# Values and gate of a retention layer as seven block products

## The chip, the cores and the metric

The kernel is one program on one core of a Trainium2 chip. It is written instruction by instruction: each engine (TensorE, ScalarE, VectorE, GpSimd, and SyncE for loads) has a program of its own, and semaphores order them. The metric is the time on the device in microseconds. GpSimd is called POOL, VectorE DVE, ScalarE ACT and TensorE PE in the profile.

## The reference, cut to what matters

A sequence of 512 tokens of width 1024 goes through a retention layer, an attention layer and a third block of pooling, neighbourhood attention and a large MLP. The change is in the first layer:

```python
def _retention_layer(x, w_in, w_out):
    hproj = x @ w_in                       # 512 x 1024 by 1024 x 6144
    q, k = 4 heads of 256 each; v, gate = 4 heads of 512 each
    q = _rope(q); k = _rope(k) * DK_A ** -0.5
    o = _chunkwise_retention(q, k, v)      # causal scores times a decay, times v
    o = (o - mean(o)) * rsqrt(var(o) + 1e-5)
    return (o * silu(gate)) @ w_out
```

The kernel computes each float32 product as three matmuls: both operands are split into a high part, rounded to the format TensorE takes, and a low part, the remainder; then high times high, high times low and low times high are added up (`split_dots`, L565 to L569).

## The kernel before

**A head.** Weights come as panels of 128x2048 floats, six a head: query, key, two of values, two of gate (`split_hi`, `split_lo`; `A0 + 0` to `A0 + 5`). SyncE loads a panel into `stage[p % 2]` (L580). ScalarE rounds it in two halves of 128x1024 into `whi` (L1458), once TensorE has finished the panel before the last, which lay in the same buffer; GpSimd subtracts and writes the remainder `wlo` (L724). TensorE's program for a head: the query product and the key product (48 matmuls of 512 columns each), the values (`token_tiles`, 96), the scores (24, of 512 to 128 columns), the first half of the gate (48), the inner products scores times values (30), the second half of the gate (48), and 16 transposes of the normalised result. Gate and result meet after the transposes, with features on partitions.

**VectorE in a head**, in this order: turning of the query by the rotary tables (`work`, four products with a PSUM source L2399 to L2402, one subtraction L2404 and one addition L2405 with both sources in SBUF), remainders of the rounded query `qk_lo`, the same for the key, remainders of the values, scores times decay (L2417), remainders of the scores `s_lo`, gate (L2426), statistics (L2433 to L2438), normalisation (L2447), products with the gate (L2452). Remainders are all recorded at L2082, roundings by ScalarE at L1461.

**Behind the heads** comes the output layer AO, which already goes by seven block products of two steps each, d = 0 to 13 (`seven`, 24 matmuls each). Its weight sums are made in DRAM by GpSimd's adding DMAs (`sum_step`) upon copies that ScalarE's queue issues (`copy_blocks`). Remainders of its steps 0 and 1 are GpSimd's work (L758, L765), of all later ones VectorE's. Then the layer norm, and the rest of the kernel, which the change leaves as it is but for the copies and sums that prepare the MLP's weights (`copy_b11`, `copy_b22`, `up_sum`).

The order of work on every engine is the order of the program; nothing is planned at run time. An engine that waits for a semaphore holds back all that stands behind it in its program.

## Time and profile before

| | |
|---|---|
| median of 3 runs | 1414.61 us (1414.3 to 1414.74) |
| the profiled execution | 1414.12 us, its span 1412.3 us |
| TensorE busy (matmul) | 1393.4 us, 99% |
| VectorE busy | 919.2 us, 65% |
| ScalarE busy | 698.8 us, 49% |
| GpSimd busy | 388.2 us, 27% |
| granted TensorE clock, mean | 0.997 |
| first layer's heads | 19.2 to 319.4 us |

A busy share is of the whole span. A matmul of 512 columns stands with 0.39 us in the timeline, since matmuls overlap; what it costs is the distance from its start to that of the next. "x2" in a timeline is two instructions merged, with the time of both; what stands in brackets is the idle time before and what ended it.

### The profile page before, as it was taken

What the parts mean: (1) busy time and instruction counts of PE and PEld (TensorE: products, weight loads), DVE (VectorE), ACT (ScalarE), POOL (GpSimd) and SP (SyncE); (2) the same over time, 40 slices, a digit from 0 to 9 for tenths busy, and PEclk for the clock granted to TensorE, in tenths of its full rate; (3) what the DMA queues carried; (4) which work ended last, traced back from release to release, by engine and by line L of the source; (5) the groups of instructions that cost most, each with busy time, mean ns of one, the idle gap of its engine ahead of it and who ended that gap; (6) DMA issues with size and microseconds to landing.
All of it is one profiled execution on the core that took longest, in us unless ns stands there. A gap on an engine that the chain in (4) does not pass through costs nothing.

```text
span 1412.3 us, 19358 instructions
## 1 busy us (share of the span) xinstructions
PE 1393.4 (99%) x7412; PEld 1203.4 (85%) x7412; DVE 919.2 (65%) x1562; ACT 698.8 (49%) x1131; POOL 388.2 (27%) x192
## 2 busy tenths in 40 slices
PE   9999999999999999999999999999999899999998
PEld 7888888888889888888888888778888899998887
DVE  6444354549961865545544479946877878789896
ACT  4323232236554533443443356648956465666554
POOL 5334254541034343343334230035314100000000
PEclk9999999999999999999999999999999999999999
DMA  7257946946533988975796557353122576446552
GB/s 292 90 194 204 296 155 164 263 115 258 188 103 129 289 235 221 312 176 157 210 302 161 162 207 284 135 193 126 64 83 75 165 184 173 128 173 213 197 187 111
DMA packets 53890, 260.26 MB, mean 184 GB/s; under 512 B 5568, under 2 KB 10304, under 8 KB 28224
## 3 DMA queue, kind: packets, MB, share of 16 engines
q1 hardware_dynamic: 37152, 163.04, 33.3%
q0 software_dynamic: 5760, 41.95, 14.9%
q10 hardware_dynamic: 10912, 54.40, 11.3%
q8 instruction: 41, 0.67, 0.2%
q14 instruction: 25, 0.20, 0.0%
HBM read 252.03 MB, written 91.23 MB: 243 GB/s over the span
## 4 chain that ended last, share of the span: by engine, by line
PE 89%; DVE 7%; ACT 2%; POOL 1%; issue 1%; DMA 0%; SPq 0%; DVEq 0%; ACTq 0%; POOLq 0%
PE bank L567 23%; PE bank L569 23%; PE bank L568 23%; PE bank L1176 6%; PE bank L1238 4%; PE bank L1127 3%; PE bank L1155 1%; DVE wlo L2082 1%; DVE wlo_a L2082 1%; DVE xlo L2082 1%; DVE br_lo L2082 1%; PE bank L1318 0%; PE bank L913 0%; PE bank L1015 0%; DMA stage<-in_w 0%
## 5 line engine op out<-in xcount | busy, mean ns | idle before, releaser
L724 POOL TENSOR_TENSOR wlo<-stage,whi 128x1024 fp32r<-128x1024 f32 (+2 forms) x116 | 291.9, 2543 | 544.8 <-ACT whi L1458 544.8
L1458 ACT ACTIVATE whi<-stage 128x1024 fp32r<-128x1024 f32 (+2 forms) x120 | 122.2, 1069 | 87.3 <-PE bank L569 64.3
L567 PE MATMUL bank<-xhi,whi 128*128 128x512 f32 (+1 forms) x428 | 149.3, 349 | 3.2 <-DVE xlo L2082 1.8
L569 PE MATMUL bank<-xhi,wlo 128*128 128x512 f32 (+1 forms) x428 | 148.5, 347 | 0.0
L568 PE MATMUL bank<-xlo,whi 128*128 128x512 f32 (+1 forms) x428 | 148.3, 346 | 0.0
L1461 ACT ACTIVATE whi<-stage 128x1024 fp32r<-128x1024 f32 (+2 forms) x125 | 118.0, 989 | 40.3 <-PE bank L569 29.4
L2082 DVE TENSOR_TENSOR wlo<-stage,whi 128x1024 fp32r<-128x1024 f32 x108 | 123.4, 1168 | 14.7 <-ACT whi L1461 14.7
L567 PEld LDWEIGHTS bank<-xhi,whi 128*128 128x128 f32 x428 | 81.1, 189 | 13.5 <-issue 2.2
L567 PE MATMUL bank<-whi,xhi 128*128 128x512 f32 (+1 forms) x236 | 91.4, 387 | 1.1 <-POOL wlo L724 1.1
L569 PE MATMUL bank<-whi,xlo 128*128 128x512 f32 (+1 forms) x236 | 90.4, 383 | 0.0
L568 PE MATMUL bank<-wlo,xhi 128*128 128x512 f32 (+1 forms) x236 | 90.3, 383 | 0.0
L569 PEld LDWEIGHTS bank<-xhi,wlo 128*128 128x128 f32 x428 | 81.0, 189 | 10.3
L568 PEld LDWEIGHTS bank<-xlo,whi 128*128 128x128 f32 x428 | 81.1, 189 | 9.8
L2082 DVE TENSOR_TENSOR wlo_a<-stage,whi_a 128x1024 fp32r<-128x1024 f32 (+1 forms) x60 | 71.4, 1217 | 18.5 <-ACT whi_a L1461 18.5
L1461 ACT ACTIVATE whi_a<-stage 128x1024 fp32r<-128x1024 f32 (+1 forms) x56 | 53.8, 1008 | 22.8 <-PE bank L569 19.9
L567 PEld LDWEIGHTS bank<-whi,xhi 128*128 128x128 f32 x236 | 44.8, 190 | 10.4 <-POOL wlo L724 1.3
L569 PEld LDWEIGHTS bank<-whi,xlo 128*128 128x128 f32 x236 | 44.7, 190 | 8.4
L568 PEld LDWEIGHTS bank<-wlo,xhi 128*128 128x128 f32 x236 | 44.9, 190 | 8.0
L1176 PE MATMUL bank<-xhi,whi 128*128 128x512 f32 x128 | 50.7, 396 | 0.0
L1176 PE MATMUL bank<-xhi,wlo 128*128 128x512 f32 x128 | 50.0, 391 | 0.0
L1176 PE MATMUL bank<-xlo,whi 128*128 128x512 f32 x128 | 49.9, 390 | 0.0
L2082 DVE TENSOR_TENSOR pt_lo<-bank,pt_hi 128x384 fp32r<-128x384 f32 (+1 forms) x48 | 26.6, 595 | 34.9 <-ACT pt_hi L1461 34.9
(451 smaller groups left out, 3943.5 us busy)
## 6 DMA issues: line engine op xcount, KB each, us to landing
stage<-in_w SPq DMA_DIRECT2D x79, 1024.0 KB, 4.9
tsum<-in_w ACTq DMA_DIRECT2D x32, 1024.0 KB, 14.5
stage<-tsum SPq DMA_DIRECT2D x32, 1024.0 KB, 4.8
tsum<-in_w POOLq DMA_DIRECT2D x16, 1024.0 KB, 10.1
tsum<-tsum POOLq DMA_DIRECT2D x16, 1024.0 KB, 10.1
stage<-in_w SPq DMA_DIRECT2D x8, 1152.0 KB, 6.3
usum<-in_w POOLq DMA_DIRECT2D x8, 1024.0 KB, 9.9
stage<-usum SPq DMA_DIRECT2D x32, 256.0 KB, 3.8
```

What stands on the lines that cost most here:

```text
L567: pe.matmul(dst, a_hi, b_hi, start=start, stop=False)
L568: pe.matmul(dst, a_hi, b_lo, start=False, stop=False)
L569: return pe.matmul(dst, a_lo, b_hi, start=False, stop=stop)
L724: pool.tensor_tensor(lo[:, r], stage[p % 2][:, r], hi[:, r].bitcast(F32), ALU.subtract).then_inc(w_lo, 1)
L1127: last = pe.matmul(bank[4 + q][:, 0:w], left, right, start=i == 0, stop=i == 4)
L1155: last = pe.transpose(dst[min(kt, 2)][:, at:at + P], prob[:, src:src + P], ident[:, :])
L1176: last = pe.matmul(bank[0][:, :], left[:, k, f], right[:, k, :], start=i == 0, stop=i == 23)
L1238: last = pe.matmul(bank[m][:, :], left[:, k, m * P:(m + 1) * P], right[:, k, :], start=i == 0, stop=i == 23)
L1458: act.activation(parts(p)[0][:, r], stage[p % 2][:, r], ACT.Copy).then_inc(w_hi, 1)
L1461: act.activation(dst, src, ACT.Copy, scale=scale).then_inc(signal, 1)
L2082: dve.tensor_tensor(dst, src, hi.bitcast(F32), ALU.subtract).then_inc(signal, 1)
```

## The change

The values and the gate of a head are one product of x (512x1024) with a 1024x1024 weight, values on the left and gate on the right. The change cuts x into blocks of 256 tokens by 512 inputs and the weight into blocks of 512x512: B11 and B21 (values), B12 and B22 (gate). Seven block products take the place of eight: with B11 and B21 directly, with B22, and with four sums T1 = B12 - B11, T3 = B22 - B12, T2 = B22 - T1, T4 = B21 - T2. The four sums of x that they need (`operand_sums`) are made once, in head 0. A block product is 24 matmuls of 512 columns.

- Per head VectorE makes the four weight sums, 128x2048 each, and the remainders of T1 to T4; GpSimd makes those of query, B11, key, B21 and B22. Products are combined by VectorE in `kept1` and `gate`, now with tokens on partitions.
- TensorE's order in a head: B11, key, B21, B22, scores (last block first), T1, T2, T3, T4, inner products, query of the next head, transposes. The last head's transposes come behind step 1 of AO.
- The gate is multiplied in with the centring of the result (`onorm`); ScalarE then scales by the root, and copies the transposed result out.
- The loads follow the new order and new places (`a_stage`); loops over heads are written out; the copies and sums in DRAM are spread otherwise: `copy_b22` goes one by one behind steps 4 to 11 of AO, `up_sum` behind AO's step 1, and the load of x to the last head. ScalarE rounds AO's first two operands within the last head, ahead of T3.

Core of the diff (TensorE's head first):

```diff
+            def head(h):
+                if h:
+                    pe.wait_ge(a_c, 12 * h)
+                block_product(h, A_B11, X)
+                turned_product(h, AK)
+                pe.wait_ge(a_k1, 2 * h + 2)
+                block_product(h, A_B21, X, True)
+                pe.wait_ge(a_q32, 4 * h + 3)
+                if h == 0:
+                    pe.wait_ge(vs_l, 1)
+                block_product(h, A_B22, Y)
                 pe.wait_ge(a_qklo, 4 * h + 4)
+                if h:
+                    pe.wait_ge(a_ot, 4 * h)
+                for kt in S_ORDER:
...
+                pe.wait_ge(a_vlo, 4 * h + 2)
+                if h == 0:
+                    pe.wait_ge(vs_l, 4)
+                block_product(h, A_T1, X)
+                pe.wait_ge(a_dec, 4 * h + 2)
+                block_product(h, A_T2, Z)
+                pe.wait_ge(a_dec, 4 * h + 4)
+                block_product(h, A_T3, W)
+                pe.wait_ge(a_c, 12 * h + 4)
+                block_product(h, A_T4, X)
...
+                pe.wait_ge(a_slo, 4 * h + 4)
+                pe.wait_ge(a_c, 12 * h + 6)
+                inner(0, (0,))
+                inner(1, (0, 1))
+                inner(2, (0, 1))
+                inner(3, (0, 1))
+                pe.wait_ge(a_vlo, 4 * h + 3)
+                inner(2, (2,))
+                pe.wait_ge(a_vlo, 4 * h + 4)
+                inner(3, (2, 3))
...
+            for h in range(HA):
+                head(h)
+                if h + 1 < HA:
+                    pe.wait_ge(a_c, 12 * h + 10)
+                    turned_product(h + 1, AQ)
+                    turn_head(h)
```

GpSimd and ScalarE:

```diff
+            for h in range(HA):
+                for j in BY_POOL:
+                    if (h, j) == (0, AQ):
+                        continue
+                    head_lo(h, j)
...
+            operand_lo(AO, 0)
+            operand_lo(AO, 1)
             weights_lo(AO, 0)
...
+                head_hi(h, AK, (a_ld[1], 32 * h + 16), (a_qk, 4 * h + 2))
+                if h:
+                    turned_out(h - 1)
...
+                head_hi(h, A_B21, (a_ld[3], 16 * h + 16), (a_m, 7 * h + 1))
+                if h == 0:
+                    operand_sum_hi(3, 3)
...
+                head_hi(h, A_B22, (a_ld[0], 32 * h + 32), (a_qk, 4 * h + 4))
...
+                if h == HA - 1:
+                    act.wait_ge(a_ot, 4 * h)
+                    operand_hi(AO, 0)
+                    operand_hi(AO, 1)
+                head_hi(h, A_T3, (g_sum, 3 + 4 * h + 2), (a_m, 7 * h + 4))
...
+                tanh(0)
+                tanh(1)
+                if h + 1 < HA:
+                    head_hi(h + 1, AQ, (a_ld[0], 32 * h + 48), (a_m, 7 * h + 6))
```

VectorE:

```diff
+                rope(h, 0)
+                if h == 0:
+                    operand_sums()
+                rope_lo(h, 0)
+                if h == 0:
+                    for n in range(4):
+                        operand_sum_lo(n)
+                rope(h, 1)
+                t1()
+                rope_lo(h, 1)
+                for q in range(2):
+                    v_low(q, X[q][:, :])
+                both(A_T1)
+                t3()
+                dve.wait_ge(g_dlo, 8 * h + 2)
+                dve.tensor_tensor(s0, s2, s0, ALU.subtract).then_inc(g_sum, 1)
...
+                for i in range(TT):
+                    decays(h, i)
...
+                both(A_T2)
...
+                dve.tensor_tensor(s0, a_staged(h, A_B21), s0, ALU.subtract).then_inc(g_sum, 1)
+                both(A_T3)
...
+                for a in range(2):
+                    dve.tensor_tensor(kept1[:, a, :], kept1[:, a, :], Z[a][:, :], ALU.add).then_inc(a_c, 1)
...
+                both(A_T4)
...
                 gates(0)
                 gates(1)
+                dve.wait_ge(a_m, 7 * h + 7)
+                for a in range(2):
+                    dve.wait_ge(a_c, 12 * h + a + 7)
+                    dve.tensor_tensor(kept1[:, a, :], kept1[:, a, :], X[a][:, :], ALU.add).then_inc(a_c, 1)
+                for q in range(2, TT):
+                    dve.wait_ge(a_c, 12 * h + 9 + q)
+                    v_low(q, kept1[:, q - 2, :])
+                gates(2)
+                gates(3)
+                if h == HA - 1:
+                    combine(AO, 2)
...
+                for q in range(TT):
+                    dve.scalar_tensor_tensor(out=onorm[:, q, :], in0=B[q][:, :], scalar=mv[:, q, 0:1],
+                                             in1=gate[:, q, :], op0=ALU.subtract, op1=ALU.mult).then_inc(a_on, 1)
```

Here `rope` is the turning with its four products, subtraction and addition, `both` the two halves of a panel's remainders, and `head_hi` waits for a load or a sum and for TensorE, then rounds a panel.

## Rows read from the trace of the kernel before

**Rows 1.** TensorE's waits: the longest in 0 to 325 us, and the longest of the run.

```profile
PE bank L1025 <- ACT xhi L1461: 1.6, 1, 1.6
...
PE bank L913 <- DVE h_tok L2263: 2.0, 1, 2.0
```

**Rows 2.** TensorE's timeline: start us, us, engine, line, operation.

```profile
107.91 0.39 PE L567 MATMUL bank<-whi,xhi 128*128 128x512 f32 x1
...
129.67 0.39 PE L567 MATMUL bank<-qk_hi 128*128 128x512 f32 x1
...
133.44 0.44 PE L567 MATMUL bank<-xhi,whi 128*128 128x512 f32 x1
...
330.40 0.39 PE L567 MATMUL bank<-whi_a,s_hi 128*128 128x512 f32 x1
```

**Rows 3.** A stretch of heads 1 and 2: busy us of each engine, TensorE clock, DMA.

```profile
core 0: us, PE busy (x) PEld busy (x) DVE busy (x) ACT busy (x) POOL busy (x), PEclk, DMA share, GB/s
...
150.00:200.00 50.00, 50.00 (x231) 41.56 (x230) 25.17 (x34) 14.34 (x18) 20.50 (x9) 1.00 0.68 233
```

**Rows 4.** VectorE's timeline, turning queries in heads 0, 1 and 2.

```profile
21.94 0.69 DVE L2404 TENSOR_TENSOR work<-work 128x512 f32<-128x512 f32 x1
22.55 0.69 DVE L2405 TENSOR_TENSOR work<-work 128x512 f32<-128x512 f32 x1
...
97.23 0.69 DVE L2399 TENSOR_TENSOR work<-bank,rope_a 128x512 f32<-128x512 f32 x1 [8.98 <-PE bank L569]
...
99.75 1.64 DVE L2404 TENSOR_TENSOR work<-work 128x512 f32<-128x512 f32 x1
101.31 2.88 DVE L2405 TENSOR_TENSOR work<-work 128x512 f32<-128x512 f32 x1
...
175.03 0.69 DVE L2399 TENSOR_TENSOR work<-bank,rope_a 128x512 f32<-128x512 f32 x1 [8.98 <-PE bank L569]
```

**Rows 5.** GpSimd's timeline in head 1.

```profile
98.43 5.21 POOL L724 TENSOR_TENSOR wlo<-stage,whi 128x1024 fp32r<-128x1024 f32 x2 [7.50 <-ACT whi L1458]
...
120.19 4.77 POOL L724 TENSOR_TENSOR wlo<-stage,whi 128x1024 fp32r<-128x1024 f32 x2 [4.89 <-ACT whi L1458]
```

**Rows 6.** VectorE's timeline near 1092 us.

```profile
1091.93 1.22 DVE L2082 TENSOR_TENSOR s2u_lo<-hid,s2u_hi 128x1024 fp32r<-128x1024 f32 x1
1093.12 3.36 DVE L2082 TENSOR_TENSOR dr_lo<-hid,dr_hi 128x1024 fp32r<-128x1024 f32 x1
1096.41 3.40 DVE L2082 TENSOR_TENSOR xlo<-hid,xhi 128x1024 fp32r<-128x1024 f32 x1
```

**Rows 7.** GpSimd's timeline, the same stretch.

```profile
1092.14 3.26 POOL L849 TENSOR_TENSOR hid<-hid 128x1024 f32<-128x1024 f32 x1 [2.49 <-DVE hid L2287]
```

**Rows 8.** VectorE's timeline in a layer norm.

```profile
400.58 2.03 DVE L2256 SCALAR_TENSOR_TENSOR xres<-oT,small,rows 128x1024 f32<-128x1024 f32 x1
```

**Rows 9.** GpSimd's timeline, the same stretch.

```profile
395.78 5.75 POOL L724 TENSOR_TENSOR wlo<-stage,whi 128x1024 fp32r<-128x1024 f32 x2 [70.45 <-ACT whi L1458]
```

**Rows 10.** VectorE's timeline, undisturbed instructions of 128x1024.

```profile
336.99 1.22 DVE L2082 TENSOR_TENSOR wlo<-stage,whi 128x1024 fp32r<-128x1024 f32 x1
338.12 1.21 DVE L2097 TENSOR_TENSOR oT<-oT 128x1024 f32<-128x1024 f32 x1
```

**Rows 11.** ScalarE's groups, 0 to 420 us: count, busy us, mean ns.

```profile
L1458 ACT ACTIVATE whi<-stage 128x1024 fp32r<-128x1024 f32 x50 | 50.1, 1053 | 68.6 <-PE bank L569 59.4 <-DMA stage<-in_w 6.2 <-issue 3.0
```

**Rows 12.** Panel loads of L580, 0 to 60 us: issue to landing.

```profile
DMA to landing us min/median/max: 4.8/5.0/10.4
```

**Rows 13.** VectorE's timeline, statistics and normalisation of head 1.

```profile
151.42 0.70 DVE L2433 BATCH_NORM_STATS2 stat<-bank 128x6 f32<-128x512 f32 x1 [2.02 <-PE bank L569]
...
153.81 2.97 DVE L2447 TENSOR_SCALAR work<-bank,mv,small 128x512 f32<-128x512 f32 x4
```

**Rows 14.** TensorE's timeline, its first matmuls.

```profile
1.47 3.78 PE L982 MATMUL bank<-qk_lo 128*128 128x512 f32 x8 [1.47 <-DVE qk_lo L2371]
5.09 0.91 PE L1025 MATMUL bank<-xhi,whi 128*128 128x512 f32 x2
```

More of the change, by code:

```diff
@@ L336, in program @@
         a_on = sem("a_on")
+        a_m = sem("a_m")
         a_t = sem("a_t")
@@ new lines, in turned_product @@
+            def turned_product(h, j):
+                wh, wl = [w.rearrange("p (k n) -> p k n", k=KX) for w in a_parts(h, j)]
+                if h and j == AK:
+                    pe.wait_ge(a_ot, 4 * h - 2)
+                for m in range(2):
+                    c = slice(m * P, (m + 1) * P)
+                    for k in range(KX):
+                        if m == 0 and k in (0, KX // 2):
+                            head_need(h, j, k > 0)
+                        last = split_dots(pe, (W if j == AQ else Y)[m][:, :], wh[:, k, c], wl[:, k, c], xhi[:, k, :],
+                                          xlo[:, k, :], k == 0, k == KX - 1)
+                    last.then_inc(a_qk, 1)
@@ new lines, in block_product @@
+            def block_product(h, j, banks, onto=False):
+                wh, wl = [w.rearrange("p (k n) -> p k n", k=PK) for w in a_parts(h, j)]
+                x_hi, x_lo = a_operand(j)
+                for kk in range(PK):
+                    if kk % 2 == 0:
+                        head_need(h, j, kk > 0)
+                    for a in range(2):
+                        r = slice(a * P, (a + 1) * P)
+                        last = split_dots(pe, banks[a][:, :], x_hi[:, kk, r], x_lo[:, kk, r], wh[:, kk, :], wl[:, kk, :],
+                                          kk == 0 and not onto, kk == PK - 1, onto)
+                last.then_inc(a_m, 1)
@@ L1623, in _, with head_hi @@
             act.wait_ge(f_hi, 5)
-            act.sem_inc(w_hi, 2)
-            split_hi(A0 + 1)
-            act.wait_ge(xt_lo, KX)
-            act.dma_start(xres[:, :, :], t["x"]).then_inc(aux["x"], 16)
+            act.sem_inc(g_hi, 2)
             A, B, E, O = bank[0:4], bank[4:8], bank[0::2], bank[1::2]
-            def head(h, last=False):
-                n = 6 * h
-                act.wait_ge(a_dec, 4 * h + 4)
+            X = bank[0:2]
+            def head_hi(h, j, ready, count):
+                act.wait_ge(*ready)
+                act.wait_ge(*count)
+                for b in range(2):
+                    r = slice(b * PAN // 2, (b + 1) * PAN // 2)
+                    copy(a_parts(h, j)[0][:, r], a_staged(h, j)[:, r], g_hi)
@@ new lines, in head @@
+                head_hi(h, A_B22, (a_ld[0], 32 * h + 32), (a_qk, 4 * h + 4))
+                for m in range(2, 4):
+                    act.wait_ge(a_q32, 4 * h + (m + 1))
+                    copy(qk_hi[:, m, :], work[:, m % 2 * 2, :], a_qkhi)
+                for q in range(2):
+                    act.wait_ge(a_m, 7 * h + 2)
+                    copy(v_hi[:, q, :], X[q][:, :], a_vhi)
+                head_hi(h, A_T1, (g_sum, 3 + 4 * h + 1), (a_m, 7 * h + 2))
+                copy_step(h, 0)
@@ new lines, in rope_lo, with head_lo @@
+            def rope_lo(h, a):
+                for m in range(2):
+                    dve.wait_ge(a_qkhi, 4 * h + (2 * a + m + 1))
+                    lo_of(qk_lo[:, 2 * a + m, :], work[:, 2 * m, :], qk_hi[:, 2 * a + m, :], a_qklo)
+            def head_lo(h, j, b):
+                hi, lo = a_parts(h, j)
+                r = slice(b * PAN // 2, (b + 1) * PAN // 2)
+                dve.wait_ge(g_hi, 2 * (SPLITS * h + j) + b + 1)
+                lo_of(lo[:, r], a_staged(h, j)[:, r], hi[:, r], g_dlo)
```

473 lines of the change are left out of this document (290 added, 183 removed).

## The prediction

> **What bounds the kernel now.** I read the waits of TensorE first, then its own pace, then what shares its time in the first layer, then the queues that would have to carry the new work. In the first 325 us TensorE waits for another engine only in its first ten microseconds, and over the whole run its longest stop later on is 2.0 us, at a transpose [rows 1]. So it runs back to back through all four heads. Its pace: from 107.91 to 129.67 us lie the 96 matmuls of one head's values, 21.76 us, 0.2267 us each [rows 2]. Beside it VectorE is busy 25.2 of 50 us in a head and GpSimd 20.5 [rows 3]. By these shares there is room for more work on both. The shares hide one thing, though, and the forecast hangs on it.
>
> **GpSimd and VectorE exclude each other.** Undisturbed, a VectorE instruction of 128x512 with both sources in SBUF costs what one with a PSUM source costs, 0.69 us at a pitch of 0.6 (head 0: L2404 at 21.94, L2405 at 22.55; L2399, from PSUM, also 0.69). But in head 1 L2404 starts at 99.75 and takes 1.64, L2405 takes 2.88 [rows 4], while GpSimd runs two subtractions from 98.43 to 103.64 [rows 5]. Undisturbed, two such subtractions take 4.77, so 2.38 each [rows 5]. 98.43 + 2.38 = 100.81, plus 0.6 gives L2404's end (101.39); GpSimd's second then runs to 103.64, plus 0.55 gives L2405's end (104.19). The four products ahead of them, with a PSUM source, don't wait: they fill 97.23 to 99.75. The order of turns is seen best at 1092 us: GpSimd becomes ready at 1092.14 inside a VectorE instruction, gets its turn when that ends (about 93.0), runs 2.38 to 95.40 [rows 7]; VectorE's next, issued at 1093.12, takes 3.36, which is the wait to 95.40 and 1.1 of work, and the one behind it 3.40, for the same reason [rows 6]. So: whole instructions, in turn, and each two-SBUF instruction that VectorE comes to while GpSimd has work waits for the rest of GpSimd's instruction, up to 2.38. scalar_tensor_tensor does it too: L2256, 128x1024 at 400.58, takes 2.03, GpSimd's second subtraction ending at 401.53 [rows 8, 9]; undisturbed that size takes 1.2 [rows 10].
>
> **What the change removes.** Values and gate of a head are 192 matmuls (8 input tiles x 3 split terms x (4 + 4)). Seven block products of 4 x 2 x 3 = 24 are 168. 24 fewer, four heads, 0.2267 us: **21.8 us** less on TensorE. Query, key, scores (3.77 us, 129.67 to 133.44), inner products and transposes keep their counts [rows 2]. With nothing late the output layer's third step (d = 2), which now begins at 330.40 [rows 2], would begin at 308.6, and the kernel would take 1414.6 - 21.8 = 1392.8.
>
> **What it adds, per head.** VectorE: four sums of 128x2048 with both sources in SBUF; eight halves of remainders of 128x1024, pitch 1.13 (336.99 to 338.12) [rows 10]; twelve block additions, 0.60; less four gated products, since the gate now goes in with the normalisation. No instruction of 2048 is in the trace: 1.13 less 0.60 is 0.53 per 512, so an estimate of 2.20, not over 2 x 1.13 = 2.26 and not under 2.1. That is 8.8 + 9.1 + 7.2 - 2.4 = 22.7 us, and 17.9 of them need both SBUF sources. ScalarE: six more halves of rounding at 1.0, two copies, four scalings, four copies out [rows 11]: 12 us on an engine that is busy 14 of 50 [rows 3]; not a bound. GpSimd: ten halves instead of twelve. Loads: as many panels; they land 5.0 us after their issue [rows 12], and in the walk below a load of 9 us makes nothing late, so they count nothing. Once, in head 0: four sums and four remainders of x, 8 x 1.13 = 9.1 us, both sources in SBUF, ahead of the turning of the keys.
>
> **The walk.** I lay each queue out in program order with these pitches and the turns above. Times of heads 1 and 2 count from the start of the head's first block product. Key product over at 16.3; VectorE's four products to 19.0. ScalarE has meanwhile rounded B22's weights, and GpSimd takes their remainders 17.6 to 20.0 and 20.6 to 23.0; VectorE's subtraction fits between, its addition ends at 23.6. B22's product needs the subtraction (20.6), and TensorE arrives at 21.8: no stop. Sum T1 to 25.8, key remainders to 27.0 (scores due 27.2), value remainders 28.2, T1's remainders 29.4 and 30.5 (the first due 31.0), sums T3 and T2 34.9, four decays 36.5, first half of T2's remainders 37.6. TensorE was due there at 36.4: **stop of 1.4**. Second half, score remainders, sum T4, first half of T3's remainders: 43.7 against 43.2 due: **0.7**. T4 is in time. Then GpSimd takes the next head's query weights, 52.5 to 57.9; the two gates, both sources in SBUF, wait 1.8 and 2.4 for it and end at 58.5; the last block additions, ScalarE's rounding and the value remainders end at 60.5, where TensorE ran out at 59.5: **1.1**. So 3.1 a head: a period of 72.3 + 3.1 = 75.4 where it is now 77.8 (97.23 to 175.03, the same instruction a head apart) [rows 4].
>
> **Head 0.** From the end of the query product at 19.2 VectorE must do 2.5 (turning) + 1.2 + 4.5 (sums of x) + 1.2 + 4.5 (remainders of x) + 2.5 + 0.6 = 17.0 before the keys' first result. In that stretch GpSimd has six halves (K, B21, B22), and each finds a two-SBUF instruction waiting: 1.2 + 5 x 2.38 = 13.1. The result is there at 49.7, TensorE arrives at 19.2 + 21.8 = 41.0: **stop of 8.8** at B22, then 0.6 (T3) and 1.1 (inner): 10.5. **Head 3** has the 3.1, and two things of its own. ScalarE now rounds two operands of the output layer ahead of T3, and GpSimd takes their remainders (39.8 to 45.2) just where VectorE has its last score remainder and the fourth sum: both wait, 4.8 more at T3. And GpSimd's remainders of the output layer's first panels hold the gates; normalisation, which now is followed by a scaling, takes 5.4 from the last statistics to its end (151.42 to 156.78) [rows 13]: the moved transposes wait 2.8. Sum of stops: 10.5 + 3.1 + 3.1 + 3.1 + 4.8 + 2.8 = **27.4**.
>
> **The sum.** 27.4 - 21.8 = 5.6; laid out in full, the output layer's third step begins at 335.8 instead of 330.4, 5.4 later. From there the work is the same and TensorE hardly waits [rows 1], so nothing gives it back. The uncertain terms: a sum of 2.15 or 2.30 instead of 2.20 moves the total by -0.8 or +1.6; GpSimd at 2.30 or 2.45 by -2.1 or +1.8; gates that don't wait by -7.
>
> **Clock.** Two of these stops, 8.8 and 5.4, are longer than any in the trace. After its first idle TensorE's first eight matmuls took 0.45 us each up to 5.09 and its next 0.23 [rows 14], that is the 1.2 and the 2.4 GHz level; after stops of up to 2.0 us there is no such stretch. If each long stop brings one, it costs 0 to 8 x 0.225 = 1.8; much of it is taken back, since the next stops wait for VectorE, which goes on. I take 0.5 in all, the ends being 0 and 3.6. By the Trainium skill, "TensorE: Matmul & The Clock Gate", "The HAM clock gate", an idle array falls to half rate and must be busy again to regain it, so both stops would cost, and the time would be 1422 rather than 1420.5; no row of this trace has a stop long enough to say.
>
> **Forecast.** The profiled execution is 1414.12 us, 1412.3 of them span, 0.5 under the median of 1414.61. Plus 5.9: 1420.0 for a profile, **1420.5** for the median.
>
> **Rivals.** (1) *Fewer stops.* The stops rest on instructions of two engines meeting. Should the gates miss GpSimd's turns (-7), and the operands in head 3 be handled before the score remainders queue (-4.8), the time is 1420.5 - 11.8 = 1408.7; it decides once the stops sum to less than 21.8. For it: shifts of 1 us move a meeting. Against it: two halves of 2.38 follow each other and leave little room to miss. 0.20. (2) *No meeting costs anything*, as the busy shares suggest: 1392.8. Against it: [rows 4 to 9]. 0.05. (3) *More is late.* Each long stop costs its full 1.8, the start's loads (three panels queued at once) come late, or the output layer, which ScalarE now also loads with eight issues of copies, starves once: 1424 to 1430. 0.12. (4) The walk as told, within 4 us: 0.63, of which 0.10 lies within 0.2% (2.8 us, about what can be told from no change) of the present time.
>
> So faster 0.25, same 0.10, slower 0.65. The range takes in (4), most of (1), and the lower half of (3): 1405 to 1426.
>
> **What would show it.** 168 block matmuls a head at 0.227. In head 0 a wait of TensorE of 8 to 9 us at B22, on VectorE's subtraction; VectorE's sums of x taking 3.5 instead of 1.2. In heads 1 and 2 a period of 75.4, stops of 1.4, 0.7, 1.1 at T2, T3 and inner products. In head 3 a stop near 5 at T3 and near 3 at the transposes. Wrong, if VectorE's two-SBUF instructions keep their 1.2 beside GpSimd, if head 0's stop at B22 is under 5, or if a stage behind the output layer changes its length.

## The result and the profile after

The changed kernel takes 1425.59 us (median; 1423.83 to 1426.73) where the kernel before, on the same chip, takes 1414.45 (1411.76 to 1414.74): a ratio of 1.008, 95% interval 1.0068 to 1.0093. Its profiled execution has a span of 1423.2 us, against 1412.3. So TensorE does 96 matmuls less and the kernel is 11 us slower. The forecast was 1420.5: right in sign. The time lies 0.4 us under the range's upper end (1426) and 1.1 outside the 4 us that the walk gave itself, where rival 3 ("more is late", 1424 to 1430, chance 0.12) stood.

First TensorE's waits in the changed kernel over the whole run, the counterpart of [rows 1] (line <- releaser: us in total, times, longest), then the single ones in the timeline of heads 0, 1 and 3 and of the output layer's end (start, us, engine, line, operation, idle before and its releaser).

```profile
PE bank L613 <- DVE work L2602: 8.0, 1, 8.0
PE bank L1000 <- DVE xres L2457: 5.7, 2, 4.1
PE bank L613 <- DVE wlo L2283: 5.3, 7, 1.2
PE bank L1167 <- ACT onorm L1614: 2.3, 1, 2.3
PE bank L613 <- DVE v_lo L2283: 2.2, 3, 1.3
```

```profile
48.34 0.80 PE L613 MATMUL bank<-whi,vs_b 128*128 128x512 f32 x1 [7.98 <-DVE work L2602]
138.73 0.47 PE L613 MATMUL bank<-whi,vs_a 128*128 128x512 f32 x1 [0.99 <-DVE wlo L2283]
144.81 0.47 PE L613 MATMUL bank<-whi,vs_b 128*128 128x512 f32 x1 [0.40 <-DVE wlo L2283]
161.24 0.50 PE L613 MATMUL bank<-v_hi,s_hi 128*128 128x512 f32 x1 [0.50 <-DVE v_lo L2283]
...
301.62 0.47 PE L613 MATMUL bank<-whi,xhi 128*128 128x512 f32 x1 [1.15 <-DVE wlo L2283]
313.36 0.50 PE L613 MATMUL bank<-v_hi,s_hi 128*128 128x512 f32 x1 [1.26 <-DVE v_lo L2283]
328.88 3.56 PE L1167 MATMUL bank<-ident,onorm 128*128 128x128 f32 x16 [2.30 <-ACT onorm L1614]
...
396.89 1.09 PE L1000 MATMUL bank<-ident,xres 128*128 128x128 f32 x8 [1.59 <-DVE xres L2457]
404.84 1.97 PE L1000 MATMUL bank<-ident,xres 128*128 128x128 f32 x8 [4.09 <-DVE xres L2457]
```

The block products stop where the walk had them: B22 in head 0 (7.98), T2, T3 and inner products in head 1 (0.99, 0.40, 0.50). Two stops at the layer norm, 5.7 us, were not in the forecast's sum.

To see where the 11 us lie I cut the first part at TensorE's own marks, read from its timeline: its first block product, the first one of each head, the output layer's third step (d = 2), and the first transposes of c_tok in the latent layer. us from mark to mark; the experiments below use the same cuts.

```
kernel      start  head 0  head 1  head 2  head 3 to d=2  d=2 to c_tok  c_tok at
before        -      -       -       -     (d=2: 330.40)     101.72      432.12
after       18.44   82.57   74.95   75.01      81.21         110.84      443.02
e1_zeros    17.89   72.14   72.23   72.27      76.85         110.16      421.54
e3_order    19.59   79.87   74.97   74.99      81.21         109.14      439.77
e4_fill     19.81   90.35   74.95   75.02      80.91         109.68      450.72
e9_fill     18.28   82.32   74.98   75.01      79.62         109.34      439.55
e2_copies   19.20   83.09   74.96   74.97      95.07         107.89      455.18
e10_copies  18.97   82.52   74.96   75.00      81.15         104.93      437.53
e11_turn    18.03   82.70   74.97   74.99      79.62         107.39      437.70
e7_early    20.43   81.72   72.54   72.56      77.90         109.17      434.32
e6_gates    18.87   81.81   74.17   74.19      75.56         110.90      435.50
e5_late     18.76   81.27   74.96   74.97      81.29         109.86      441.11
e12_best    18.46   79.04   72.24   72.26      72.27         103.90      418.17
e13_spaced  17.79   79.54   72.23   72.27      72.23         103.87      417.93
```

The changed kernel reaches d = 2 at 332.18, only 1.8 us later than before; between d = 2 and c_tok it loses another 9.1; from c_tok to the end both take 980.18 (1423.2 - 443.02, 1412.3 - 432.12). The start moves by up to 2.6 us from one profile to another, whatever the edit, so the columns to its right are the better measure of it. Head 0 moves as well: in the six profiles that leave it as it is (after, e2, e5, e7, e10, e11) it takes 81.27 to 83.09. A difference of a few tenths in that column tells nothing.

### The profile page after: what moved, and what is told of

The parts are those of the page before. It is cut to its first block, busy times and chain, and to the rows that moved or that the text cites. A ratio compares the mean times of both kernels' runs of the same rounds, so it can differ in the third digit from the quotient of the medians.

```text
span 1423.2 us, 19150 instructions
## 1 busy us (share of the span) xinstructions
PE 1380.3 (97%) x7316; PEld 1189.0 (84%) x7316; DVE 1036.6 (73%) x1650; ACT 745.0 (52%) x1197; POOL 377.8 (27%) x184
## 4 chain that ended last, share of the span: by engine, by line
PE 70%; DVE 22%; ACT 3%; issue 2%; DMA 2%; POOL 1%; SPq 0%; DVEq 0%; ACTq 0%; POOLq 0%
PE bank L613 18%; PE bank L615 18%; PE bank L614 18%; PE bank L1329 6%; DVE wlo L2283 4%; PE bank L1391 3%; PE bank L1280 3%; DVE gate L2651 1%; DMA stage<-in_w 1%; PE bank L1308 1%; DVE wlo_a L2283 1%; DVE s_lo L2283 1%; DVE work L2603 1%; DVE xlo L2283 1%; DMA v_spill<-v_tok 1%
## 5 line engine op out<-in xcount | busy, mean ns | idle before, releaser
L792 POOL TENSOR_TENSOR wlo<-stage,whi 128x1024 fp32r<-128x1024 f32 (+2 forms) x70 | 175.9, 2538 | 379.9 <-ACT whi L1611 332.4
L1614 ACT ACTIVATE whi<-stage 128x1024 fp32r<-128x1024 f32 (+2 forms) x155 | 148.1, 1001 | 82.2 <-PE bank L615 61.8
L613 PE MATMUL bank<-xhi,whi 128*128 128x256 f32 (+1 forms) x300 | 98.9, 330 | 3.2 <-DVE xlo L2283 1.8
L615 PE MATMUL bank<-xhi,wlo 128*128 128x256 f32 (+1 forms) x300 | 98.6, 329 | 0.0
L614 PE MATMUL bank<-xlo,whi 128*128 128x256 f32 (+1 forms) x300 | 98.6, 329 | 0.0
L841 POOL TENSOR_TENSOR wlo<-stage,whi 128x1024 fp32r<-128x1024 f32 x22 | 58.5, 2682 | 106.0 <-ACT whi L1614 106.0
L1611 ACT ACTIVATE whi<-stage 128x1024 fp32r<-128x1024 f32 (+2 forms) x74 | 76.1, 1079 | 19.4 <-issue 14.3
L1614 ACT ACTIVATE whi_a<-stage 128x1024 fp32r<-128x1024 f32 (+1 forms) x56 | 53.8, 1008 | 23.3 <-PE bank L615 20.1
L613 PEld LDWEIGHTS bank<-xhi,whi 128*128 128x128 f32 x300 | 57.1, 190 | 8.7 <-issue 2.2
L614 PEld LDWEIGHTS bank<-xlo,whi 128*128 128x128 f32 x300 | 57.1, 190 | 5.0
L615 PEld LDWEIGHTS bank<-xhi,wlo 128*128 128x128 f32 x300 | 57.1, 190 | 5.0
L1614 ACT ACTIVATE whi<-oT 128x1024 fp32r<-128x1024 f32 x34 | 34.1, 1051 | 44.5 <-DVE oT L2686 28.3
```

The costliest lines, as they stand in the source:

```text
L613: pe.matmul(dst, a_hi, b_hi, start=start, stop=False, skip_group_check=onto)
L614: pe.matmul(dst, a_hi, b_lo, start=False, stop=False, skip_group_check=onto)
L615: return pe.matmul(dst, a_lo, b_hi, start=False, stop=stop, skip_group_check=onto)
L792: pool.tensor_tensor(lo[:, r], stage[p % 2][:, r], hi[:, r].bitcast(F32), ALU.subtract).then_inc(w_lo, 1)
L841: pool.tensor_tensor(lo[:, r], a_staged(h, j)[:, r], hi[:, r].bitcast(F32), ALU.subtract).then_inc(g_plo, 1)
L1611: act.activation(parts(p)[0][:, r], stage[p % 2][:, r], ACT.Copy).then_inc(w_hi, 1)
```

## Experiments

The edits are shown shortened: waits that only go with a moved piece of work are left out.

**Do the two engines exclude each other?** GpSimd still waits and signals, but writes zeros.

```
 def head_lo(h, j):                      # GpSimd
-    pool.tensor_tensor(lo[:, r], a_staged(h, j)[:, r], hi[:, r].bitcast(F32), ALU.subtract).then_inc(g_plo, 1)
+    pool.memset(lo[:, r].bitcast(F32), 0.0).then_inc(g_plo, 1)
```

> In the four heads GpSimd writes zeros into the weights' remainder tiles instead of subtracting (the low parts of B11, keys' panel, B21, B22 and the later heads' query panel are left out of the result); it still waits for the rounding and still signals, but it reads nothing of SBUF. Theory (GpSimd and VectorE instructions with two SBUF operands exclude each other in turns): VectorE's gate products (128x512, 2060 ns on the mean in the changed kernel) and the sums inside the rotation (work<-work, 2609 and 1558 ns) fall to the 0.7 us that their like with one PSUM operand take, so the stop of 8.0 us ahead of head 0's fourth block falls under 2 us, the stops of about 1.9 to 2.6 us a head at T2, T3 and the inner products go, and the output layer's third step starts 15 to 24 us earlier than the 332.18 us of the changed kernel: total 1402 to 1412 us. Rival (VectorE simply has more work than the time between the keys and the fourth block gives): the mean durations stay above 1.5 us, the stop stays at 6 us or more, total 1422 to 1427 us.

Measured 1405.98 us, ratio to before 0.9946 (0.9931 to 0.9961). Groups of VectorE's and GpSimd's instructions (busy us, mean ns of one): first the changed kernel from 100 to 320 us, then e1_zeros over the same stretch, then its GpSimd from 20 to 320.

```profile
L2651 DVE SCALAR_TENSOR_TENSOR gate<-th,gate 128x512 f32<-128x512 f32 x12 | 23.7, 2013 | 0.0
L2603 DVE TENSOR_TENSOR work<-work 128x512 f32<-128x512 f32 x6 | 17.3, 2883 | 0.0
L2602 DVE TENSOR_TENSOR work<-work 128x512 f32<-128x512 f32 x6 | 9.8, 1634 | 0.2
```

```profile
L2650 DVE SCALAR_TENSOR_TENSOR gate<-th,gate 128x512 f32<-128x512 f32 x12 | 13.8, 1187 | 0.0
L2601 DVE TENSOR_TENSOR work<-work 128x512 f32<-128x512 f32 x5 | 3.5, 692 | 0.2
L2602 DVE TENSOR_TENSOR work<-work 128x512 f32<-128x512 f32 x5 | 3.4, 685 | 0.0
```

```profile
L841 POOL MEMSET wlo<- 128x1024 f32 x36 | 34.3, 956 | 171.6 <-ACT whi L1613 171.6
```

The sums of the rotation fall from 2883 and 1634 ns to 685 and 692; the stop at B22 is gone (no such row among its waits), and heads 0 to 2 take 72.1 to 72.3 us each, the walk's period without stops. Only head 3's gates stay slow (three of its four, 2.3 to 2.9 us): there GpSimd still subtracts the output layer's panels. The rival (too much work for VectorE) falls: its work is the same here. One reservation: zeros are also written faster (956 ns) than remainders are computed, so GpSimd is relieved in time as well; but no wait of TensorE for GpSimd was among the stops, and e6_gates below moves the gates alone, with GpSimd's subtractions as they are. The Trainium skill ("SBUF — State Buffer", "Who interferes with whom") says that a VectorE instruction with two inputs in SBUF contends with a GpSimd instruction that reads SBUF, not with one that only writes it; this run agrees.

**Head 0's stop.** Its queue on VectorE, in order:

```
 if h == 0:
-    for n in range(4): operand_sum_lo(n)
+    operand_sum_lo(0)
 rope(h, 1); t1(); rope_lo(h, 1)
+if h == 0: operand_sum_lo(2); dve.wait_ge(vs_l, 2)
 v_low(0); v_low(1)
+if h == 0: operand_sum_lo(1)
 ...                                      # operand_sum_lo(3) ahead of both(A_T3)
```

> In head 0 VectorE computes only the first remainder of the operand sums ahead of the keys' rotation; the other three follow it, each ahead of the remainders of the weight sum that it is multiplied with. Theory (the fourth block's stop of 8.0 us in head 0 is VectorE's queue ahead of the keys' rotation, four remainders among it): three subtractions of 1.5 to 3 us leave that path, the stop falls to 1 to 4 us, some 2 to 4 us of it come back as later stops at T1, T2 and T3 of head 0; total 1421 to 1424 us. Rival (the stop hangs on the rotation's own instructions in turn with GpSimd alone): the stop stays over 6 us and the total within 1 us of 1425.6.

Measured 1422.73 us, 1.007 (1.0054 to 1.0085). B22's stop falls to 0.27 us, the block starts 22.2 us into the head instead of 29.9, and T1 now waits 0.74 and T2 2.56: of 7.7 us head 0 keeps 2.7; 5.0 come back, more than the 2 to 4 expected. The theory on the stop is right; VectorE is busy from the first rotation up to T4, so order alone moves little of it.

**Is the half-rate stretch a cost of its own?** In the changed kernel, from 44 us on (window: PE, PEld, DVE, ACT, POOL busy, granted clock, DMA share, GB/s):

```profile
44.00:48.00 4.00, 0.00 (x0) 0.00 (x0) 3.96 (x6) 0.00 (x0) 0.09 (x1) 0.69 0.00 0
48.00:52.00 4.00, 3.65 (x9) 2.92 (x10) 4.00 (x5) 3.08 (x5) 0.00 (x0) 0.50 0.00 0
```

In the stop the clock falls to its 1.2 GHz level (0.50), and B22's 24 products take 7.47 us for 5.44. I filled the stop with products for nobody, first behind the wait for the rotated keys, by mistake:

```
 pe.wait_ge(a_q32, 4 * h + 3)
+if h == 0:
+    for i in range(32): pe.matmul(W[0][:, :], xhi[:, 0, 0:P], xhi[:, 0, :], start=True, stop=True)
 if h == 0: pe.wait_ge(vs_l, 1)
```

> 32 products of 512 columns into a free bank fill TensorE's stop of 8.0 us ahead of head 0's fourth block (nothing of the result changes). Theory (the half-rate stretch from 48 to 52 us follows from the idle time and is a cost of its own): the granted clock stays at full rate from 40 to 60 us and the total falls by 1 to 2.5 us, to 1423 to 1424.5 us. Rival (after the stop VectorE sets the pace up to the next heads, or the clock dips for another reason): the total stays within 0.7 us of 1425.6, or the 0.50 windows stay.

Measured 1432.78 us, 1.0131 (1.0115 to 1.0146). TensorE's wait of 7.8 us still stands ahead of them, at the first added product, so they filled nothing and added themselves. The half-rate stretch now lies in them: B22 starts 9.8 us later in the head and takes 2.0 less (5.44), so head 0 grows by 7.8. What the clock costs without them this run doesn't tell. The second attempt has 34 of them ahead of that wait, behind a wait for the free bank (a_q32 at 2).

> 34 products of 512 columns into a free bank now stand ahead of TensorE's wait for the rotated keys, so that they lie in the stop of head 0 (34 x 0.2267 = 7.7 us of its 8.0; e4_fill had them behind that wait, where they only added themselves). Theory (the half-rate stretch from 48 us follows from the stop): the 24 products of the fourth block take 5.4 us instead of 7.5, nothing stops TensorE again before the next head, so the gain of 2.0 us reaches the output layer: its third step at 330.0 to 331.0 us, total 1423 to 1424.5 us. Rival (VectorE sets the pace of head 0 after the block, so the 2.0 us come back as stops at T1, T2 or T3): total within 0.5 us of 1425.6.

Measured 1422.47 us, 1.0062 (1.0049 to 1.0075). Its window:

```profile
48.00:52.00 4.00, 3.34 (x15) 2.74 (x15) 4.00 (x5) 2.73 (x5) 0.00 (x0) 1.00 0.00 0
```

Full rate: B22's products take 5.6 us, and the scores start 1.4 us earlier in the head. Of this 0.9 is left at T3 and 0.25 at the head's end (82.32 for 82.57), by new stops of 0.33 at T3 and 0.49 in the inner products, each for VectorE. The 0.25 is less than head 0 moves by itself, and VectorE released B22 0.5 us later in this head (30.41 for 29.90). Counted from B22's first product to the next head it is 51.91 for 52.67: the half rate costs 0.76 us of the 1.89 that B22's products got back, and the rest returns as stops. In the six profiles with head 0 unchanged B22 takes 7.0 to 8.35 us, and from its end to the next head it is 45.20 to 45.26 in each: there all of B22's length reaches the head's end. So the rival is right in part: VectorE sets the pace of head 0 only once B22 takes less than some 6.7 (51.91 - 45.20). The total fell mostly for another reason, in 2 places that the edit doesn't touch: the transposes of head 3, and the stretch after the layer norm's stop, ran at half rate for a shorter time (1.6 and 1.5 us in the table). The last section comes back to that.

**The output layer.** It loses 9.1 us. ScalarE's rounding there, with waits that the kernel before doesn't have (ACT L1614, idle before and its releaser), and the end of VectorE's queue with GpSimd's two remainders:

```profile
366.26 1.06 ACT L1614 ACTIVATE whi<-stage 128x1024 fp32r<-128x1024 f32 x1 [5.35 <-DMA stage<-in_w]
384.06 2.01 ACT L1614 ACTIVATE whi<-stage 128x1024 fp32r<-128x1024 f32 x2 [1.53 <-DMA stage<-tsum]
```

```profile
392.78 0.68 DVE L2437 SCALAR_TENSOR_TENSOR xres<-xres,bank 128x512 f32<-128x512 f32 x1
...
395.55 1.28 DVE L2457 SCALAR_TENSOR_TENSOR xres<-oT,small,rows 128x1024 f32<-128x1024 f32 x1
...
401.39 3.40 DVE L2457 SCALAR_TENSOR_TENSOR xres<-oT,small,rows 128x1024 f32<-128x1024 f32 x1
```

```profile
401.36 5.65 POOL L792 TENSOR_TENSOR wlo<-stage,whi 128x1024 fp32r<-128x1024 f32 x2 [47.48 <-DVE wlo_a L2283]
```

From d = 2 to the first gathering (L2437) VectorE takes 60.6 us; before, 55.5 (385.88 - 330.40). Then GpSimd's remainders begin 0.03 us ahead of the second shift, which takes 3.40 for 1.28; before, the shift at 394.50 was over when GpSimd began at 395.78 [rows 9]. First the transfers:

```
-if 4 <= d < 12: copy_b22(d - 4)             # ScalarE, output layer
+copy_b22(2 * k); copy_b22(2 * k + 1)        # ScalarE, head 3, after each of T1 to T4 (k = 0 to 3)
-for g in range(4): up_sum(0, g)             # GpSimd, output layer
+up_sum(0, ...) twice after AK, twice after A_B21   # GpSimd, head 3
```

> The eight copies of the up layer's B22 blocks and the four additions onto its sums, which the change put into the output layer's stretch, go back into head 3 (two copies after each rounding T1 to T4, additions after the keys' and B21's remainders). Theory (these DRAM transfers hold up the output layer's weight loads, so ScalarE and VectorE reach its gathering late, so TensorE stops for 1.6 and 4.1 us at the layer norm's transposes and then runs at half rate): both stops fall under 1 us in sum, no window at 0.50 follows at 400 to 410 us, total 1416 to 1419 us. Rival (VectorE is late there because of its own queue of remainders and gathers, as the changed start of the layer leaves it): the two stops stay at 5 us or more, total within 1.5 us of 1425.6; or the copies cost the same in head 3.

Measured 1436.48 us, 1.0157 (1.0143 to 1.0171): slower, by the edit's own fault. TensorE waits 1.76 us for GpSimd's B21 remainders and 11.28 for those of B22, which stood behind the additions. GpSimd's queue in head 3:

```profile
257.11 0.81 POOL L817 DMA_DIRECT2D usum<-in_w  x1
267.18 0.84 POOL L817 DMA_DIRECT2D usum<-in_w  x1 [9.26 <-issue]
...
275.31 0.82 POOL L817 DMA_DIRECT2D usum<-in_w  x1 [2.56 <-issue]
284.02 0.83 POOL L817 DMA_DIRECT2D usum<-in_w  x1 [7.89 <-issue]
284.57 5.15 POOL L841 TENSOR_TENSOR wlo<-stage,whi 128x1024 fp32r<-128x1024 f32 x2
```

Each issue starts 8 to 10 us after the one before it, and the remainders stand behind it. The output layer itself is 2.95 us shorter, and VectorE takes 57.5 to its first gathering; but a stop of 2.89 is left, with half rate behind it, where under 1 and full rate were expected. e10_copies keeps the copies in head 3 and puts the additions, in pairs, behind the remainders of panels B0 + 1 and B0 + 2.

> The eight copies of the up layer's B22 blocks are issued in head 3 by ScalarE, as in e2_copies, but the four additions by GpSimd stand behind the latent layer's first panels, in nobody's way (e2_copies' own wait for the earlier sums, ahead of B21's remainders, cost TensorE 13.0 us). Theory (the transfers in the output layer's stretch make VectorE late there by 3.1 of the 5.1 us, by the spans from its third step to the first gathering: 60.6 us in the changed kernel, 57.5 in e2_copies, 55.5 before): the stops at the layer norm fall from 5.7 to about 3 us, total 1421.5 to 1424 us. Rival (the copies cost as much in head 3 by delaying its weights): TensorE waits for remainders of B11, keys or B21 in head 3 and the total is 1425 us or more.

Measured 1422.24 us, 1.0063 (1.005 to 1.0076). The theory is right, on the layer: ScalarE waits for no weight load there, the stretch is 104.93, 5.9 shorter (3.2 of it VectorE's earlier gathering, the rest that only one stop is left, of 3.0, with the clock at full rate after it). But 2.2 of it are lost right behind c_tok, where TensorE waits 0.94 and 0.69 us for GpSimd's remainders, held behind a pair of additions. Whether the copies or the additions held the layer up was not separated. Then the turn:

```
 pool.wait_ge(w_lo, 2 * (B0 + 1))
+pool.wait_ge(n_x, 2)                        # the second tile's shift is done
 for p in range(B0 + 1, M0 - 1): split_lo(p)
```

> GpSimd waits with its remainders at the first layer norm until VectorE has finished the second token tile's shift. Theory (in the changed kernel GpSimd's two subtractions at 401.36 us start 0.03 us ahead of VectorE's shift at 401.39, which then takes 3.40 us for 1.28; before, VectorE's started first and paid nothing): the shift takes 1.28 us, the second stop at the layer norm falls from 4.1 to 2.0 us, the half-rate stretch behind it (2.7 us dearer than before) stays or goes: total 1420.5 to 1423.5 us. Rival (the order of the two there costs nothing on the path): within 0.7 us of 1425.6.

Measured 1422.74 us, 1.006 (1.0048 to 1.0072). The shift, in the timeline of VectorE:

```profile
399.97 1.28 DVE L2458 SCALAR_TENSOR_TENSOR xres<-oT,small,rows 128x1024 f32<-128x1024 f32 x1
```

1.28 us, the stop falls from 4.09 to 2.0, the clock stays at 1.00 behind it, the stretch is 107.39, 3.45 shorter. Theory right; a new wait of 0.67 us for GpSimd's later remainders is the price.

The totals of e3, e9, e10 and e11, each alone, lie 2.9 to 3.4 us under the changed kernel's, and their intervals touch its own (1.0068 to 1.0093); what they show rests on the rows. The next two lie clearly under it.

**Heads 1 to 3.** T1 and T3 ahead of the keys' rotation, where VectorE waits for TensorE:

```
+if h: t1(); t3()
 rope(h, 1)
-t1()
+if h == 0: t1()                             # t3() likewise
```

> In heads 1 to 3 VectorE computes the weight sums T1 and T3 ahead of the keys' rotation (in head 0 as it is). Theory (VectorE idles 6.5 us a head ahead of that rotation, waiting for TensorE, while its queue behind it is what TensorE waits for at T2, T3 and the inner products): 4.6 us of its work leave the loaded stretch, the stops of 1.9 us in heads 1 and 2 and of 6.1 us in head 3 shrink, the output layer's third step starts at 324 to 328 us instead of 332.18, total 1417 to 1421.5 us. Rival (the sums then delay the rotation and with it scores and fourth block): TensorE stops ahead of the fourth block in heads 1 to 3, total 1424 us or more.

Measured 1419.03 us, 1.0037 (1.0024 to 1.0049). Heads 1 and 2 take 72.54 and 72.56: no stop is left in them. Nothing stops at the fourth block. The gain is 2.4 us a head, slack of VectorE used. Head 3 gains 3.3, of which 1.6 is that its transposes run at full rate, behind a stop of 1.50. And it has a new stop at T3, of 2.09, the very one that the prediction had forecast there (VectorE, GpSimd, TensorE):

```profile
281.91 3.91 DVE L2283 TENSOR_TENSOR s_lo<-work,s_hi 128x128 fp32r<-128x128 f32 x4
285.74 4.48 DVE L2704 TENSOR_TENSOR oT<-gate,oT 128x2048 f32<-128x2048 f32 x1
```

```profile
282.64 5.43 POOL L833 TENSOR_TENSOR ar_lo<-oT,ar_hi 128x1024 fp32r<-128x1024 f32 x2 [12.36 <-ACT ar_hi L1614]
```

```profile
291.50 0.47 PE L613 MATMUL bank<-whi,vs_b 128*128 128x512 f32 x1 [2.09 <-DVE wlo L2283]
```

```
-gates(0); gates(1)                          # VectorE, ahead of the wait for T4's product
 ...
 for q in (2, 3): v_low(q, kept1[:, q - 2, :])
+gates(0); gates(1)
 gates(2); gates(3)                          # ScalarE: v_hi of 2 and 3 ahead of tanh(2), tanh(3)
```

> Alone on the changed kernel: VectorE takes the remainders of the values' third and fourth tile ahead of all four gate products, ScalarE rounds these values ahead of the last two tanh. Theory (inner products of tiles 2 and 3 wait for those remainders, behind gate products of 2060 ns each): the stops of 0.5, 0.5 and 1.3 us inside the inner products go, head 3's turned tiles gain nothing: total 1422.5 to 1424.5 us. Rival (the remainders are late through T4's combination, not through the gates): within 0.7 us of 1425.6.

Measured 1417.82 us, 1.0026 (1.0014 to 1.0038): 7.8 us, four times the expectation. VectorE and GpSimd in head 1, first the changed kernel:

```profile
153.98 5.14 DVE L2651 SCALAR_TENSOR_TENSOR gate<-th,gate 128x512 f32<-128x512 f32 x2
...
165.84 2.16 DVE L2743 TENSOR_SCALAR small<-mv 128x4 f32<-128x4 f32 x1
```

```profile
153.36 5.21 POOL L841 TENSOR_TENSOR wlo<-stage,whi 128x1024 fp32r<-128x1024 f32 x2 [9.38 <-ACT whi L1614]
163.22 4.75 POOL L841 TENSOR_TENSOR wlo<-oT,whi 128x1024 fp32r<-128x1024 f32 x2 [4.65 <-ACT whi L1614]
```

and with the edit, where the gates lie behind GpSimd's query panel (153.03 to 157.80):

```profile
158.87 1.28 DVE L2651 SCALAR_TENSOR_TENSOR gate<-th,gate 128x512 f32<-128x512 f32 x2
160.31 1.29 DVE L2651 SCALAR_TENSOR_TENSOR gate<-th,gate 128x512 f32<-128x512 f32 x2 [0.16 <-ACT th L1849]
...
164.46 0.17 DVE L2743 TENSOR_SCALAR small<-mv 128x4 f32<-128x4 f32 x1
```

The twelve gates of heads 1 to 3 fall from 2013 to 683 ns. While VectorE waits for T4's product (1.97 us) GpSimd takes its turn for nothing. In head 3 the gates, the sum behind them and with them the normalisation come earlier, so d = 2 comes 5.65 us earlier in the head: the stops of 1.26 and 2.30 are gone, and 1.6 more is that the transposes run at full rate (1.67 us to d = 2 for 3.30). My expectation had looked at the inner products only.

```
-operand_hi(AO, 0); operand_hi(AO, 1)        # ScalarE in head 3, ahead of T3's rounding
 head_hi(h, A_T3, ...); head_hi(h, A_T4, ...)
+operand_hi(AO, 0); operand_hi(AO, 1)
```

> Alone on the changed kernel: in head 3 ScalarE rounds the output layer's first two operands after T4's weights instead of ahead of T3's. The prediction had put a stop of 4.8 us at T3 down to these two roundings and GpSimd's two remainders; the trace shows 0.39 us at T3 and 1.15 at T4. Theory now: only the 1.15 us at T4 belong to them: total 1424 to 1425.5 us. Rival (the 2.3 us at head 3's transposes and the inner stop of 1.3 go with them too): 1421 to 1423 us.

Measured 1425.56 us, 1.0079 (1.0064 to 1.0095): no gain. Head 3 up to d = 2 takes 81.29 for 81.21. T4's remainders on VectorE grew from 4.53 to 6.25 us, as GpSimd's operands met them there. The stop at T4 is 0.91 in two parts for 1.15, the one at the transposes 0.68 for 2.30, but the one in the inner products 2.92 for 1.26. So these roundings cost the head nothing that a later place saves.

**All together.** e12_best takes e3, e5, e6, e7, e10 and e11 at once.

> All orders that helped at once, on the changed kernel: head 0's operand remainders spread (e3_order), T1 and T3 ahead of the keys' rotation in heads 1 to 3 (e7_early), the up layer's copies in head 3 and its additions behind the latent panels (e10_copies), GpSimd's turn at the layer norm (e11_turn), and in each head the value remainders ahead of the gate products, in head 3 the output layer's operands rounded after T4. Theory (TensorE's 96 products fewer are worth 21.8 us and what took them back was order alone): stops up to the output layer's third step fall from about 18 us to 6 to 10, that step starts at 318 to 323 us instead of 332.18, the layer norm's stops fall by 3 to 5 us: total 1404 to 1411 us, faster than before the change. Rival (each remedy uses the same slack of VectorE, so that they do not add): 1413 us or more.

Measured 1406.38 us, 0.9942 (0.9929 to 0.9956). Heads 1 to 3 are free of stops (72.24, 72.26, 72.27), head 0 has 79.04, the output layer 103.90: the remedies add. TensorE's largest new waits are for GpSimd's remainders:

```profile
422.63 0.50 PE L613 MATMUL bank<-whi,xhi 128*128 128x512 f32 x1 [2.56 <-POOL wlo L792]
424.97 0.80 PE L613 MATMUL bank<-whi,xhi 128*128 128x512 f32 x1 [0.57 <-POOL wlo L792]
```

```
-if p == B0 + 1: up_sum(0, 0); up_sum(0, 1)
-elif p == B0 + 2: up_sum(0, 2); up_sum(0, 3)
+up_sum(0, p - B0 - 1)                       # one behind each panel, the last behind M0 - 1
```

> e12_best with GpSimd's four additions to the up layer's sums issued one behind each latent panel's remainders instead of two and two. In e12_best the second issue of each pair starts 10.5 us after the first one's and GpSimd's next remainders stand behind it: TensorE waits 2.6, 0.6 and 0.7 us for them. Theory (GpSimd, with a second transfer issued while the first runs, is held up in its own queue): the waits of 2.6 and 0.6 us go, total 1402 to 1404 us. Rival (those waits stem from the wait at the layer norm, as in e11_turn, where 0.7 us of them are seen): total within 1 us of 1406.4.

Measured **1401.13 us**, 0.9912 (0.9899 to 0.9926): 12.4 us under the kernel before, 24.5 under the changed one (23.8 by the two ratios, as they ran on different chips). The waits of 2.6 and 0.6 are gone, and with them the half rate behind them (0.50 from 424 to 428 us in e12_best). The first 50 products behind c_tok take 9.5 us for 16.05:

```profile
PE bank L613 <- DVE wlo L2288: 3.3, 2, 2.6
...
PE bank L613 <- POOL wlo L792: 0.6, 1, 0.6
```

So the seven products are worth having. Most of what took their gain back was the order of the queues. Of the 21.8 us 9.0 are still missing by the spans (1399.5 for 1412.3 - 21.8): 5.5 up to d = 2, head 0's above all (79.54 for 72.2), 2.1 to c_tok, and 1.4 behind it, where the profiles differ by up to 1.8 without an edit there.

## Why the prediction was right, and where it was not

The sign and the mechanism (VectorE and GpSimd hold each other up, and TensorE stops for it) were right. That the time still fell into the range was luck: two steps failed, in opposite directions.

- **The matmuls.** Right: 96 in 21.86 us (101.01 to 122.87), and periods of 72.2 to 72.3 us without stops.
- **Costs on VectorE.** A sum of 128x2048 takes 2.28 us at a pitch of 2.20 (131.38 to 133.58), as estimated.
- **Head 0.** 82.8 forecast, 82.57 measured. The stop is 7.98 for 8.8. By the walk's own terms (19.2 + 17.0 + 13.1 = 49.3, not 49.7) it should have read 8.3. GpSimd has the six halves, and two of the four sums of x, two of the four remainders and the last two instructions of the queries' rotation wait for them (3.3 to 3.4 us for 1.2; 1.96 and 2.88 for 0.7). The stops of 0.6 and 1.1 behind it did not come; B22 at half rate, 2.0 us longer, stands in their place. So the head's total is nearer than its parts.
- **Heads 1 and 2.** Stops of 1.4, 0.7 and 1.1 forecast, 0.99, 0.40 and 0.50 measured; the period 75.4 forecast, 74.95 and 75.01 measured. The gates do meet GpSimd. The stops are overstated by 1.2 a head, and the period by 0.4.
- **Head 3.** Here a step failed: "both wait, 4.8 more at T3". The two meet as told, but the one that waits is GpSimd:

```profile
289.61 1.69 DVE L2283 TENSOR_TENSOR s_lo<-work,s_hi 128x128 fp32r<-128x128 f32 x4
291.21 2.28 DVE L2699 TENSOR_TENSOR oT<-gate,oT 128x2048 f32<-128x2048 f32 x1
293.42 2.35 DVE L2283 TENSOR_TENSOR wlo<-stage,whi 128x1024 fp32r<-128x1024 f32 x2
295.69 1.27 DVE L2705 TENSOR_TENSOR grow<-grow,bank 128x512 f32<-128x512 f32 x2
...
298.07 4.53 DVE L2283 TENSOR_TENSOR wlo<-oT,whi 128x1024 fp32r<-128x1024 f32 x2
```

```profile
290.33 10.06 POOL L833 TENSOR_TENSOR ar_lo<-oT,ar_hi 128x1024 fp32r<-128x1024 f32 x2 [16.33 <-ACT ar_hi L1614]
```

  GpSimd is ready at 290.33, yet VectorE's next instructions with two SBUF sources, end to end up to 295.69, keep their undisturbed times. GpSimd's first subtraction takes 7.71 us and ends at 298.04: 2.35 after VectorE turns to sources in PSUM. Its second then holds T4's remainders (4.53 for 2.35), hence 1.15 at T4, and 0.39 at T3. In e7_early the same meeting, 0.19 us into the same instruction of VectorE (s_lo of 128x384) as here, went the other way: VectorE waited, 2.2 us twice, and T3 stopped for 2.09. The Trainium skill ("SBUF — State Buffer", "Who interferes with whom") has it that the issue order decides who blocks; the starts in these rows don't show it, since they stand in the same order in both runs. So "in turns" was too simple, and what decides at such a meeting stays open. The 2.8 at the transposes was 2.30. In sum, head 3 to d = 2 took 81.21 where the walk had 83.0, and with the small differences above d = 2 came at 332.18 for 335.8.
- **Behind d = 2.** The step that failed by most: "From there the work is the same and TensorE hardly waits [rows 1], so nothing gives it back". The work is not the same, as the change puts eight copies on ScalarE's queue and four additions on GpSimd's into that stretch; the prediction had named the copies, under rival 3, and put them at nothing in its sum. TensorE's ledger of the 9.1: stops of 1.59 and 4.09, and 2.8 at half rate behind the second (8 transposes in 1.62 us, before in 0.79; 12 products in 4.82, before in 2.82); the remaining 0.6 is spread thin. Behind the stops stands VectorE, 5.1 us late at its first gathering, of which the transfers make 3.1 (60.6 to 57.5), and 2.1 later still by the lost turn. What the other 2.0 hang on was not tried. The prediction's sign of being wrong (a stage behind the output layer changes its length) did not come, 980.18 in both; it did not cover the output layer itself.
- **Clock.** 0.5 assumed, 3.6 at most. In head 0 it costs 0.76 (e9_fill). At the two places behind which VectorE is not the pace it costs 1.6 (head 3's transposes, 3.30 us to d = 2 for 1.70) and the 2.8 above: 5.2 in all. The two dear ones stand behind stops of 2.30 and 4.09, not behind the two that the term was meant for. The 1422 that stands beside the forecast is not what its terms give: 1.8 for each of two stops in place of the 0.5 would be 1423.6.

So 5.9 - 3.6 (d = 2 earlier than walked) - 0.5 (the clock term, now inside the others) + 9.1 = 10.9: the measured growth of the span. The sign was right and by its reason. The size, 11.1 for 5.9 in the medians, came into the range by luck, by errors of opposite sign, and the larger one was a stretch that I had not laid out.

## What to carry to other kernels

When a change moves work between queues, walk the stage behind it too, with each DMA issue that now lies in it. Look for two-operand VectorE work that runs beside GpSimd's, and put it where GpSimd's turn falls into a time in which VectorE waits anyway. And before discarding a change that loses what it should gain, list TensorE's stops by their releaser: here a handful of changes of order, each small, gave back 24.5 us of the 32.9 (21.8 + 11.1) that had been lost.

## What the runs showed of the hardware that I had not expected

- A second DMA issue on GpSimd's queue, on the heels of the first, comes 8 to 12 us after it, and what is queued behind it stands too (e2_copies, 11.28 us on TensorE; e12_best, 2.56; spaced out, gone). In the changed kernel the four issues from 319.52 us on start 10.0, 11.4 and 12.2 us apart. These additions move 1 MB each. The first three have landed at 329.16, 340.63 and 352.78, and the next issues start at 329.51, 340.90 and 353.05; in e2_copies it is 0.3 us behind each landing as well. So the second issue seems to stand until the first transfer has landed, though the program has no such wait there; why is not shown.
- A TENSOR_SCALAR of 128x4, all in SBUF, took 2.16 us beside GpSimd's subtraction and 0.17 without. The two run in different kernels (the changed one, e6_gates), GpSimd's subtraction ending at 167.97 and VectorE's instruction at 168.00. So it isn't only instructions with two tensors that wait.
- The length of a stop doesn't settle whether TensorE's clock falls. Head 3's transposes, behind a stop of 2.3 us each time, ran at 0.50 in the changed kernel and at 1.00 in e11_turn, which doesn't touch them:

```profile
329.00:332.00 3.00, 3.00 (x15) 3.00 (x16) 3.00 (x4) 1.48 (x3) 0.84 (x1) 0.50 0.96 330
```

```profile
329.00:332.00 3.00, 3.00 (x22) 2.71 (x21) 3.00 (x3) 2.72 (x5) 0.84 (x1) 1.00 0.92 341
```

  T2's stop in head 0 of 2.56 us brought half rate in e3_order (0.50 from 62 to 64 us), one of 2.58 in e12_best did not; T3 started 48.71 us into the head in both, since VectorE was the pace. By the Trainium skill ("TensorE: Matmul & The Clock Gate", "The HAM clock gate") the gate's observation runs free of the kernel, so that where a stop falls matters; the runs fit this, but none was made to test it. Single profiles of this kernel differ by some 1.6 us at such a place.
